# A hybrid decoder layer: the selected values of the NSA pages take another way into SBUF

## The chip, the cores and the metric

One core of one Trainium2 chip runs the whole program in one launch. The metric is the device time of that launch in microseconds; lower is better.

## The reference, cut to what matters

One decoder layer is computed for a prompt group (512 tokens) and a sample group (8 sequences, one new token each, 2048 cached positions in 16 pages of 128 rows). Between two large linear layers stand four mixers. Only the native sparse attention (NSA) of the sample group is touched by the change:

```
nsa_past = cache_nsa_kv[l, page_table].reshape(bs, past_len, 4, HEAD_DIM)   # [cmp_k, cmp_v, sel_k, sel_v]
kc, vc   = nsa_compress(rows[:, :, 0] / rows[:, :, 1], ...)                  # small MLP over 32-row blocks
imp      = importance of the 64-row blocks, from the compressed branch
p2       = masked_softmax(q . sel_k of the 16 chosen blocks)
o_sel    = p2 @ sel_v                                                       # the "selected values"
```

Each sequence thus reads, through the page table, 16 pages of four vectors of 64 floats a row. The compressed keys and values and the selected keys are needed early, the selected values only once the importance is known. MoBA, the second mixer with a paged cache, reads 4 x 256 KB of pages a unit, 32 units.

## The kernel before

The work is laid out as one list of steps, `timeline()` (TL). Every engine walks that list in order and does its own share of each step, so the list sets the order on each engine and semaphores tie the engines together. Where the list is merged from several streams, each step carries a due time, and the merge sorts by it.

**Panels.** The weights come as 89 panels of 512 KB (`load_panel`, three buffers `raw`). ScalarE casts a panel to a high part (L1258), VectorE (two of them GpSimd) forms the low part (L1630), TensorE multiplies (L793) and ScalarE or VectorE takes the sums out of PSUM. Panels 0 to 16 are the combined input projection, 17 to 24 the output projection, the rest the feed-forward part.

**NSA blocks.** Behind each of the panels 5 to 12 stands one step `nsa` (b = 0 to 7). SyncE loads the 16 pages of a sequence as 16 transfers of 96 KB (rows of 768 B: compressed pair and selected keys) into one half of `nsa_ring` (`load_nsa`, L660); the load of block n waits for the scores of block n-2. TensorE does `compress` (L820) and `sel_scores` (L839), ScalarE copies the sums to `hu` (L1290, L1291), VectorE adds (L1650), takes the row maximum (L1657) and subtracts (L1662), ScalarE takes the exponentials (L1296). GpSimd computes the pooling differences (`pdiff`, behind panels 8 and 10). Behind panel 12 ScalarE also takes out two convolution results (`cpw`, L1373), for which panel 13 waits; a little later (`zcols`, L1311) it writes `Vn`, whose space the gate weights `wgate` have held before.

**The merged stretch.** Behind panel 16 the last seven MoBA pairs (9 to 15), the prompt's attention columns, the joining of the statistics and the selected values are merged by due time. A MoBA pair is scores (`mu`, L1085), transpose (`mt`, L1092) and values (`mp`, L1097). Behind `mp` of pair n, SyncE loads unit 2n+4 and GpSimd unit 2n+5 (L629, L1546) for pair n+2: four transfers of 256 KB each, rows of 2 KB, each issuer waiting for `mp_mm`. The selected values come in 32 steps `selv`, six behind each pair: four transfers of 32 KB each with rows of 256 B, half of the steps on SyncE (L707), half on GpSimd (L1554), the page numbers read into registers first. They are read from a separate tensor `selv_pages` into eight buffers `selV[b]`, and the product with the probabilities (`spv`, L1150) follows from due time 37 on. A queue works in order, so a MoBA load stands behind the selv transfers that come before it in the list.

Of the kernel before, what the change touches and what calls it, by code (L numbers as in the profile page):

```python
# [5 lines left out]
F32 = mybir.dt.float32  # L6
# [4 lines left out]
ACT = mybir.ActivationFunctionType  # L11
# [3 lines left out]
P = 128  # L15
# [88 lines left out]
ROW_PIECES = (4, 9, 9, 6)  # L104
MB1, PAIR_T, SELV_T = 9, 9.1, 6
SELV_POOL = (1, 3, 5, 7)
SELV_AT = [8 * (_m // 8) + (_m % 8) // 2 + 4 * (_m % 2) for _m in range(4 * B)]
NCN = sum(c[0] != "moba" for c in COLS)
# [9 lines left out]
def timeline():  # L118
# [119 lines left out]
    for g in range(MB1, MB):  # L238
        at_ = 1 + PAIR_T * (g - MB1)
        units += [(at_, ("mu", g)), (at_ + 2.5, ("mt", g)), (at_ + 4.7, ("mp", g))]  # L240
        units += [(at_ + 4.6 * (m >= 4), ("selv", k)) for m, k in enumerate(SELV_AT[SELV_T * (g - MB1):SELV_T * (g - MB1 + 1)])]
    end = 1 + PAIR_T * (MB - MB1)
    join = [(8 + 2 * k, ("stat", k)) for k in range(5)] + [(18.5, ("comba", 0)), (19.8, ("combe", 0)), (22.3, ("comba", 1)), (23.9, ("comba", 2)), (27.4, ("backa", 0))]
    for b in range(B):
# [111 lines left out]
def build(nc, a, o):  # L356
    ctx = ExitStack()
    with ctx:
        def sem(name):
            return ctx.enter_context(nc.semaphore(name))  # L360
# [25 lines left out]
        w1 = place("w1", [P, 16, P])  # L386
        at[0] = o_a + 16384
        nsa_ring = place("nsa_ring", [P, 2, PAGES, 192])
        o_m = at[0]
# [7 lines left out]

        selV = [place(f"selV{b}", [P, PAGES, HD], F32, o_raw + ((OUT0 + b) % NRAW if b < NRAW else b) * PAGES * HD * 4 if b < B - 1 else o_op + (KT + 6) * NT * 4) for b in range(B)]
        WB = place("WB", [B, 11, P], F32, o_op + 2 * NT * 4)

# [73 lines left out]
        Vn = place("Vn", [P, 3, QT, P])  # L474
        wgate = place("wgate", [P, KT * GW], F32, o_vn)
        zs = place("zs", [B, 12, P])
        cst = place("cst", [P, NCONST])
# [75 lines left out]
        def bank_read(eng, k, step):  # L553
# [28 lines left out]
            sem("shift_h"), sem("cq_done"), sem("cexp_done"), sem("pv_done"), sem("o_done"), sem("pick_done"))  # L582
        shift_low = sem("shift_low_done")
        pool_d, pool_mm = sem("pool_d"), sem("pool_mm")
        cm_mm, csq_done, cv_mm, cn_done, cswish, cpw_mm = (
# [6 lines left out]
            sem("ms_mm"), sem("mmax"), sem("mt_mm"), sem("mp_mm"), sem("om_done"))  # L592
        stat_mm, comb_sub, comb_exp, wb_done, back_mm = (
            sem("stat_mm"), sem("comb_sub"), sem("comb_exp"), sem("wb_done"), sem("back_mm"))
        pscaled, st_mm, spv_mm, md_done, mpv_mm, fin_o, fin_mm = (
# [16 lines left out]
        def _(sp_):  # L612
# [19 lines left out]
            for kind, n, *part in TL:  # L632
# [21 lines left out]
                elif kind == "load_nsa":  # L654
                    if n == 1:
                        sp_.wait_ge(cmp_mm, 1)
                    if n >= 2:
                        sp_.wait_ge(ssel_mm, n - 1)
                    for p, v in enumerate(pages(n * PAGES, PAGES)):
                        sp_.dma_start(nsa_ring[:, n % 2, p, :],  # L660
                                      a["nsa_pages"][bass.ds(v, 1)].rearrange("a p n -> (a p) n")).then_inc(nsa_in[n % 2], 16)
                elif kind == "load_post":
                    sp_.wait_ge(ssel_mm, B)
                    sp_.wait_ge(kc_done, B + 1)
                    sp_.wait_ge(conv_done, 1)
# [62 lines left out]
        def _(pe):  # L728
# [220 lines left out]
            for step in TL:  # L949
# [187 lines left out]
                elif kind == "spv":  # L1137

                    b = n
                    if b == 0:  # L1140
                        read(pe, ACC[max(m for m in range(NACC1) if PAIR[m] == 1)])
                        mm(psum[:, 3, :], zeros[:, :], Psel[:, 0, :], start=True, stop=False, skip_group_check=True)
                    pe.wait_ge(selv_in[b], 16 * PAGES)
                    pe.wait_ge(win_in, 32)
# [79 lines left out]
        def _(act):  # L1224
# [13 lines left out]
            for step in TL:  # L1238
# [39 lines left out]
                elif kind in ("cmpp", "nsa"):  # L1278
                    idx = 0 if kind == "cmpp" else n + 1
                    m = NCMP if idx else NCMP_P  # L1280
                    act.wait_ge(cmp_mm, idx + 1)
                    if idx == 0:
# [24 lines left out]
                elif kind == "zcols":  # L1307
                    act.wait_ge(zc_mm, 1)
                    fn(gT[:, :, :], psum[:, 4, 0:QT * NGATE].rearrange("p (a b) -> p a b", a=QT), ACT.Tanh, scale=0.5).then_inc(gate_t, 1)
                    act.wait_ge(zc_mm, 2)  # L1310
                    fn(Vn[:, 0, :, :], psum[:, 5, :].rearrange("p (a b) -> p a b", a=QT), ACT.Copy).then_inc(vn_done, 1)  # L1311
                elif kind == "zrow":
# [79 lines left out]
                elif kind == "combe" and n == 0:  # L1392
                    act.wait_ge(comb_sub, 1)
                    fn(sm[:, 0:NGATE], zs[:, 0, 0:NGATE], ACT.Tanh, scale=0.5)
                    fn(eb[:, 2, :, 0:33], eb[:, 2, :, 0:33], ACT.Exp)
                    fn(eb[:, 2, :, 50:55], eb[:, 2, :, 50:55], ACT.Exp).then_inc(comb_exp, 1)
                elif kind == "combe" and n == 1:
                    act.wait_ge(comb_sub, 2)
                    fn(eb[:, 2, :, 33:50], eb[:, 2, :, 33:50], ACT.Exp).then_inc(comb_exp, 1)
                elif kind == "backa":  # L1400
# [80 lines left out]
        def _(pool):  # L1481
# [16 lines left out]
            for kind, n, *part in TL:  # L1498
# [40 lines left out]
                if kind == "mp" and 2 * n + 5 < MU:  # L1539
# [5 lines left out]
                    for j, v in enumerate(ids):  # L1545
                        pool.dma_start(moba_ring[q % 4][:, j, :],  # L1546
                                       a["moba_pages"][bass.ds(v, 1)].rearrange("a p n -> (a p) n")).then_inc(moba_odd[q % 4 // 2], 16)
                if kind == "selv" and n // 4 in SELV_POOL:

                    if n == 4:  # L1550
                        pool.wait_ge(mm_done, N_IN_PANELS)
                    pool.wait_ge(mp_mm, MB1 + SELV_AT.index(n) // SELV_T - 1)
                    for p, v in enumerate(pool_pages(n * 4), n * 4):
                        pool.dma_start(selV[p // PAGES][:, p % PAGES, :],  # L1554
                                       a["selv_pages"][bass.ds(v, 1)].rearrange("a p n -> (a p) n")).then_inc(selv_in[p // PAGES], 16)
                elif kind == "xsum":
# [40 lines left out]
        def _(dve):  # L1597
# [22 lines left out]
            for step in TL:  # L1620
# [81 lines left out]
                elif kind == "taps_s":  # L1702
                    if n == 0:
                        tmp = Vn[:, 0, :, :].rearrange("p a b -> p (a b)")[:, 0:B * CW].rearrange("p (b k) -> p b k", b=B)
                        for t in range(2):
# [167 lines left out]
                elif kind in ("comba", "combm"):  # L1873
# [6 lines left out]
                    if n == 0:  # L1880
# [21 lines left out]
                        for br, (lo, hi) in parts:  # L1902
                            last = tt(E[:, :, lo:hi], spread(MN[:, br, :], hi - lo), NM[:, :, lo:hi], ALU.subtract)
                        last.then_inc(comb_sub, 1)
                    elif n == 1:
                        if kind == "comba":
                            dve.wait_ge(comb_exp, 1)
                            ts(sm[:, 0:NGATE], sm[:, 0:NGATE], 0.5, 0.5, ALU.mult, ALU.add)
                        else:
                            dve.wait_ge(comb_exp, 2)  # L1910
                        for br, (lo, hi) in parts:
# [185 lines left out]
def layouts(x):  # L2097
# [86 lines left out]
    for n in range(2):  # L2184
# [6 lines left out]
        "w_gate": f(np.pad(panel(w_in, allr, r(c0[3], NGATE)), ((0, 0), (0, 0), (0, GW - NGATE))).reshape(P, KT * GW)),  # L2191
        "nsa_pages": f(np.concatenate([cmpT, selK], 2)),
        "selv_pages": f(nsa[:, :, 3]),
        "moba_pages": f(np.concatenate([mK, mV], 2)),
# [39 lines left out]
```

## Time and profile before

| | us |
|---|---|
| median of 3 runs | 766.06 |
| the three runs | 765.99, 766.06, 770.39 |
| profiled execution, device time | 770.32 |
| its span, first to last instruction | 768.6 |

| engine | busy us | share |
|---|---|---|
| TensorE (PE) | 737.8 | 96% |
| VectorE (DVE) | 429.2 | 56% |
| ScalarE (ACT) | 285.5 | 37% |
| GpSimd (POOL) | 210.4 | 27% |

The chain that ended last is 76% TensorE and 5% DMA, the largest DMA part being loads of MoBA pages. 113.49 MB move in all, 17,017 of the 63,980 packets being under 512 B. A span is the time from the first to the last instruction; the device time holds a little more. A timeline row gives the start, the time, the engine and the line, and in brackets how long the engine stood before it and what ended that. In a row of windows the DMA share is that of the 16 DMA engines, and PEclk is the granted TensorE clock as a share of full speed.

### The profile page before, as it was taken

The page shows a single profiled execution, that of the slowest core. Times are in us where ns is not written, and L with a number is a line of the kernel's source. Part 1 is how long each engine was busy: PE and PEld are TensorE (multiplying, and loading weights), DVE is VectorE, ACT ScalarE, POOL GpSimd, SP SyncE. Part 2 cuts the span into 40 slices and gives each one's busy share as a digit, 9 for nine tenths or more (in the row PEclk, how much of TensorE's full clock was granted, in tenths as well). Part 3 has the DMA queues.
Part 4 walks back from the last instruction along what each step waited for, and adds up shares of the span by engine and source line. Part 5 has one row for each costly group of instructions (what it writes and reads, how often), then busy time and mean ns, then how long its engine had stood idle before and what let it go on. Part 6 is the DMA issues. An engine that isn't in the chain of part 4 may idle for free.

```text
span 768.6 us, 17343 instructions
## 1 busy us (share of the span) xinstructions
PE 737.8 (96%) x6904; PEld 659.2 (86%) x6904; DVE 429.2 (56%) x740; ACT 285.5 (37%) x561; POOL 210.4 (27%) x284
## 2 busy tenths in 40 slices
PE   8999999998987899999999999999999999999997
PEld 7999989875563545589999999999999999999996
DVE  4878994665643532556866556433563355536355
ACT  5222334465553222533434454212341124324115
POOL 0000527024226772004747721001110012100433
PEclk9999999999999899999999999999999999999999
DMA  9656773378779996321332333322233323325002
GB/s 332 188 151 182 213 200 97 133 286 315 280 252 309 261 280 208 117 83 56 130 144 84 89 104 104 117 83 84 83 104 93 106 71 95 107 87 165 2 15 99
DMA packets 63980, 113.49 MB, mean 148 GB/s; under 512 B 17017, under 2 KB 36218, under 8 KB 63226
## 3 DMA queue, kind: packets, MB, share of 16 engines
q1 hardware_dynamic: 57370, 95.58, 39.9%
q0 software_dynamic: 6528, 16.78, 6.7%
q8 instruction: 55, 0.90, 0.5%
q14 instruction: 27, 0.22, 0.1%
HBM read 107.90 MB, written 6.52 MB: 149 GB/s over the span
## 4 chain that ended last, share of the span: by engine, by line
PE 76%; DVE 8%; DMA 5%; issue 5%; SPq 4%; ACT 3%; POOL 0%; ACTq 0%; DVEq 0%; POOLq 0%
PE psum L793 55%; DMA moba_hi<-in_moba_pages 4%; PE psum L812 4%; PE psum L820 3%; PE psum L899 2%; PE psum L933 2%; SPq L707 1%; PE psum L1085 1%; SPq L629 1%; PE psum L868 1%; PE psum L1097 1%; DVE yc L1700 1%; DVE wL L1630 1%; PE psum L1133 1%; DMA wgate<-in_w_gate 1%
## 5 line engine op out<-in xcount | busy, mean ns | idle before, releaser
L1630 DVE TENSOR_TENSOR wL<-raw,wH 128x1024 fp32r<-128x1024 f32 (+1 forms) x85 | 107.1, 1261 | 84.2 <-ACT wH L1258 84.2
L1258 ACT ACTIVATE wH<-raw 128x1024 fp32r<-128x1024 f32 (+1 forms) x87 | 88.8, 1021 | 103.1 <-PE psum L793 101.1
L793 PE MATMUL psum<-oxH,wH 128*128 128x260 f32 (+1 forms) x512 | 105.0, 286 | 0.7 <-DVE oxL L2054 0.5
L793 PE MATMUL psum<-oxH,wL 128*128 128x260 f32 (+1 forms) x512 | 103.9, 284 | 0.0
L793 PE MATMUL psum<-oxL,wH 128*128 128x260 f32 (+1 forms) x512 | 103.4, 283 | 0.0
L1592 POOL TENSOR_TENSOR hsq<-relu 128x520 f32<-128x520 f32 x32 | 33.8, 1055 | 217.9 <-ACT relu L1437 217.9
L793 PE MATMUL psum<-opH,wH 128*128 128x260 f32 x400 | 85.5, 295 | 5.2 <-DVE wL L1630 1.4
L793 PEld LDWEIGHTS psum<-oxH,wH 128*128 128x128 f32 x512 | 79.5, 189 | 2.5 <-issue 1.7
L793 PE MATMUL psum<-opL,wH 128*128 128x260 f32 x400 | 80.5, 283 | 0.0
L793 PE MATMUL psum<-opH,wL 128*128 128x260 f32 x400 | 80.5, 283 | 0.0
L793 PEld LDWEIGHTS psum<-oxL,wH 128*128 128x128 f32 x512 | 79.9, 190 | 0.0
L793 PEld LDWEIGHTS psum<-oxH,wL 128*128 128x128 f32 x512 | 79.4, 189 | 0.0
L793 PE MATMUL psum<-hidH,wL 128*128 128x260 f32 x384 | 77.4, 283 | 0.0
L793 PE MATMUL psum<-hidL,wH 128*128 128x260 f32 x384 | 77.3, 283 | 0.0
L793 PE MATMUL psum<-hidH,wH 128*128 128x260 f32 x384 | 77.2, 282 | 0.0
L793 PEld LDWEIGHTS psum<-opH,wH 128*128 128x128 f32 x400 | 61.6, 189 | 11.9 <-issue 4.0
L1437 ACT ACTIVATE relu<-relu,wcol 128x520 f32<-128x520 f32 x32 | 23.4, 731 | 112.0 <-DVE relu L2002 112.0
L793 PEld LDWEIGHTS psum<-opH,wL 128*128 128x128 f32 x400 | 61.8, 189 | 0.0
L793 PEld LDWEIGHTS psum<-opL,wH 128*128 128x128 f32 x400 | 61.7, 189 | 0.0
L793 PEld LDWEIGHTS psum<-hidH,wH 128*128 128x128 f32 x384 | 59.2, 189 | 0.0
L793 PEld LDWEIGHTS psum<-hidH,wL 128*128 128x128 f32 x384 | 59.2, 188 | 0.0
L793 PEld LDWEIGHTS psum<-hidL,wH 128*128 128x128 f32 x384 | 59.0, 188 | 0.0
(395 smaller groups left out, 1313.1 us busy)
## 6 DMA issues: line engine op xcount, KB each, us to landing
raw<-in_panels SPq DMA_DIRECT2D x88, 512.0 KB, 3.6
nsa_ring<-in_nsa_pages SPq DMA_DIRECT2D x128, 96.0 KB, 2.2
moba_hi<-in_moba_pages SPq DMA_DIRECT2D x36, 256.0 KB, 5.2
moba_lo<-in_moba_pages SPq DMA_DIRECT2D x36, 256.0 KB, 5.3
moba_hi<-in_moba_pages POOLq DMA_DIRECT2D x28, 256.0 KB, 5.1
moba_lo<-in_moba_pages POOLq DMA_DIRECT2D x28, 256.0 KB, 5.5
xres<-in_xT SPq DMA_DIRECT2D x8, 260.0 KB, 5.2
xres<-in_xT SPq DMA_DIRECT2D x1, 2080.0 KB, 8.6
```

The lines of the kernel that those rows point to most:

```text
L629: sp_.dma_start(moba_ring[q % 4][:, p, :], a["moba_pages"][bass.ds(v, 1)].rearrange("a p n -> (a p) n")).then_inc(moba_in[q % 4], 16)
L707: sp_.dma_start(selV[p // PAGES][:, p % PAGES, :], a["selv_pages"][bass.ds(v, 1)].rearrange("a p n -> (a p) n")).then_inc(selv_in[p // PAG ...
L793: last = mm(out[:, hf, 0:cols], w, x[:, k, hf * HALF:hf * HALF + cols], start=(t == 0 and j == 0), stop=(t == KT - 1 and j == 2))
L812: last = mm(psum[:, q % 4, 0:HALF], w[:, t, :], x[:, t, h * HALF:(h + 1) * HALF], start=(t == 0 and j == 0), stop=(t == KT - 1 and j == 2))
L820: last = mm(psum[:, 4, kv * 256:kv * 256 + n], w1[:, kv * 8 + r, :], rhs(kv, r), start=(r == 0), stop=(r == 7))
L868: mm(psum[:, b + e, 0:m], zT[base:base + HD, sq + t, i * P:(i + 1) * P], zT[base:base + HD, sk, 0:m], start=True, stop=False, skip_group_c ...
L899: mm(out[e], k, zT[base:base + HD, sq + t, lo:T], start=True, stop=False, skip_group_check=True)
L933: last = mm(psum[base:base + HD, 6 + t, lo:T], v, PT[0:keys, n % 2, e, 0:T - lo], start=COL_FIRST[n], stop=COL_LAST[n], skip_group_check=True)
L1258: fn(wtiles(0, n).rearrange("p a b -> p (a b)")[:, cols], raw[:, n % NRAW, cols], ACT.Copy).then_inc(h_done, 1)
L1437: fn(relu[:, up_no % 2, :], relu[:, up_no % 2, :], ACT.Relu, bias=wcol[:, up_no % 3, 0:1], scale=-1.0).then_inc(relu_done, 1)
L1592: nc.gpsimd.tensor_tensor(hsq[:, up_no % 2, :], relu[:, up_no % 2, :], relu[:, up_no % 2, :], ALU.mult).then_inc(sq_done, 1)
L1630: tt(wtiles(1, n).rearrange("p a b -> p (a b)")[:, cols], raw[:, n % NRAW, cols], wtiles(0, n).rearrange("p a b -> p (a b)")[:, cols].bitc ...
```

## The change

The fourth vector of each page row, the selected value, is appended to the NSA pages, so that a row has 1 KB and a page transfer 128 KB. `nsa_ring` grows by a third, into space behind `w1` that was free. In each `nsa` step ScalarE first waits for the pages and copies the 64 value columns of all 16 pages into one of two buffers `stage` (in the space of `Vn`); GpSimd then issues one transfer of 512 KB from `stage` to a DRAM tensor `selv_rows[b]`. The next load of the same ring half waits for the copy, ScalarE's copy of block n for the write of block n-2, and `zcols` for all eight writes. In the merged stretch one step `selv` for each sequence remains, on SyncE alone: one transfer of 512 KB, rows of 4 KB, with no page numbers, due at 1, 6, 11, ..., 36. GpSimd has no selv transfers left there. The temporary of `taps_s` moves, and two semaphores of the joining become one.

```diff
-MB1, PAIR_T, SELV_T = 9, 9.1, 6
-SELV_POOL = (1, 3, 5, 7)
+MB1, PAIR_T, SELV_T = 9, 9.1, 5
...
-        units += [(at_ + 4.6 * (m >= 4), ("selv", k)) for m, k in enumerate(SELV_AT[SELV_T * (g - MB1):SELV_T * (g - MB1 + 1)])]
     end = 1 + PAIR_T * (MB - MB1)
+    units += [(1 + SELV_T * b, ("selv", b)) for b in range(B)]
...
-        nsa_ring = place("nsa_ring", [P, 2, PAGES, 192])
+        nsa_ring = place("nsa_ring", [P, 2, PAGES, 256])
...
+        selv_rows = nc.dram_tensor("selv_rows", [B, P, PAGES, HD], F32, kind="Internal").ap()
+        stage = place("stage", [P, 2, PAGES, HD], F32, o_vn)
# SyncE, load_nsa
                     if n >= 2:
                         sp_.wait_ge(ssel_mm, n - 1)
+                        sp_.wait_ge(packed, n - 1)
# SyncE, selv
-                elif kind == "selv" and n // 4 not in SELV_POOL:
+                elif kind == "selv":
                     if n == 0:
                         sp_.wait_ge(mm_done, N_IN_PANELS)
-                    for p, v in enumerate(pages(4 * n, 4), 4 * n):
-                        sp_.dma_start(selV[p // PAGES][:, p % PAGES, :],
-                                      a["selv_pages"][bass.ds(v, 1)].rearrange("a p n -> (a p) n")).then_inc(selv_in[p // PAGES], 16)
+                        for done in selv_out:
+                            sp_.wait_ge(done, 16 * B // 2)
+                    sp_.dma_start(selV[n][:, :, :], selv_rows[n]).then_inc(selv_in[n], 16)
# ScalarE, nsa
+                    if idx:
+                        act.wait_ge(nsa_in[n % 2], 16 * PAGES * (n // 2 + 1))
+                        if n == 0:
+                            act.wait_ge(gate_mm, 1)
+                        if n >= 2:
+                            act.wait_ge(selv_out[n % 2], 16 * (n // 2))
+                        fn(stage[:, n % 2, :, :], nsa_ring[:, n % 2, :, 192:256], ACT.Copy).then_inc(packed, 1)
                     act.wait_ge(cmp_mm, idx + 1)
# ScalarE, zcols, ahead of the copy to Vn
+                    for done in selv_out:
+                        act.wait_ge(done, 16 * B // 2)
# GpSimd
-                if kind == "selv" and n // 4 in SELV_POOL:
...
+                if kind == "nsa":
+                    pool.wait_ge(packed, n + 1)
+                    pool.dma_start(selv_rows[n], stage[:, n % 2]).then_inc(selv_out[n % 2], 16)
```

## Rows read from the trace of the kernel before

**Rows 1.** Page of the profiled run, its first line
```profile
span 768.6 us, 17343 instructions
```

**Rows 2.** Windows, whole core, stage of the NSA pages; span, engines, PEclk, DMA share, GB/s
```profile
67.90:78.90 11.00, 11.00 (x102) 10.10 (x101) 10.56 (x19) 3.30 (x8) 0.00 (x0) 1.00 0.70 189
```

**Rows 3.** Timeline of SyncE's queue; start us, us, engine line op
```profile
55.90 9.45 SPq L660 DMA_DIRECT2D nsa_ring<-in_nsa_pages  x16
65.41 0.42 SPq L619 DMA_DIRECT2D raw<-in_panels  x1
67.02 9.22 SPq L660 DMA_DIRECT2D nsa_ring<-in_nsa_pages  x16
```

**Rows 4.** Chain of work that ended last; start us, us, what
```profile
72.35 3.77 PE psum L820 x32
```

**Rows 5.** Timeline of ScalarE, same stage
```profile
98.21 0.27 ACT L1290 ACTIVATE hu<-psum 64x127 f32<-64x127 f32 x1 [2.90 <-PE psum L820]
...
124.40 0.27 ACT L1290 ACTIVATE hu<-psum 64x127 f32<-64x127 f32 x1 [1.07 <-PE psum L820]
...
138.49 0.68 ACT L1358 ACTIVATE zT<-psum,vec 128x520 f32<-128x520 f32 x1
139.19 0.27 ACT L1290 ACTIVATE hu<-psum 64x127 f32<-64x127 f32 x1
...
143.50 1.06 ACT L1258 ACTIVATE wH<-raw 128x1024 fp32r<-128x1024 f32 x1
...
149.79 0.60 ACT L1311 ACTIVATE Vn<-psum 128x512 f32<-128x512 f32 x1 [0.28 <-PE psum L982]
```

**Rows 6.** Timeline of VectorE, the last NSA block
```profile
139.21 0.68 DVE L1669 TENSOR_REDUCE st<-Psel 128x8 f32<-128x512 f32 x1
```

**Rows 7.** Timeline of TensorE, panel 13 begins
```profile
143.66 0.51 PE L793 MATMUL psum<-opH,wH 128*128 128x260 f32 x2 [1.19 <-ACT zT L1373]
```

**Rows 8.** Windows, three stretches with different transfers
```profile
70.00:73.00 3.00, 3.00 (x24) 2.63 (x23) 2.86 (x5) 0.61 (x3) 0.00 (x0) 1.00 0.75 203
169.00:174.00 5.00, 5.00 (x72) 3.69 (x72) 2.46 (x8) 3.23 (x12) 2.77 (x2) 1.00 1.00 357
228.00:232.00 4.00, 3.20 (x54) 1.32 (x42) 2.86 (x9) 1.51 (x5) 2.15 (x4) 1.00 0.59 121
```

**Rows 9.** Timeline of SyncE's queue behind panel 16
```profile
230.93 4.58 SPq L629 DMA_DIRECT2D moba_hi<-in_moba_pages  x4
236.55 7.62 SPq L707 DMA_DIRECT2D selV<-in_selv_pages  x12
244.68 1.88 SPq L629 DMA_DIRECT2D moba_lo<-in_moba_pages  x4
...
254.89 2.65 SPq L629 DMA_DIRECT2D moba_hi<-in_moba_pages  x4
```

**Rows 10.** Timeline of GpSimd, same stretch
```profile
242.41 2.29 POOL L1546 DMA_DIRECT2D moba_lo<-in_moba_pages  x4 [0.41 <-issue]
```

**Rows 11.** Timeline of TensorE, same stretch
```profile
233.18 1.07 PE L1097 MATMUL psum<-moba_lo,PTm 128*32 128x256 f32 x16 [0.34 <-DVE PTm L1814]
...
243.35 1.93 PE L1085 MATMUL psum<-moba_hi,QM 128*32 128x128 f32 x32 [4.12 <-DMA moba_hi<-in_moba_pages]
...
253.74 1.08 PE L1085 MATMUL psum<-moba_lo,QM 128*32 128x128 f32 x32 [0.46 <-DMA moba_lo<-in_moba_pages]
...
264.28 1.94 PE L1085 MATMUL psum<-moba_hi,QM 128*32 128x128 f32 x32 [0.62 <-DMA moba_hi<-in_moba_pages]
```

**Rows 12.** Windows around two of these waits, with the granted clock
```profile
240.00:244.00 4.00, 0.65 (x14) 0.68 (x18) 0.00 (x0) 0.00 (x0) 3.36 (x7) 0.92 1.13 231
244.00:248.00 4.00, 4.00 (x40) 1.90 (x31) 0.87 (x5) 0.46 (x2) 3.01 (x7) 0.65 0.97 275
264.00:268.00 4.00, 3.72 (x46) 2.68 (x46) 2.59 (x7) 0.81 (x3) 3.18 (x6) 0.50 0.79 206
268.00:272.00 4.00, 4.00 (x23) 1.56 (x25) 0.92 (x3) 0.22 (x1) 3.26 (x7) 0.67 0.94 318
```

More of the change, by code:

```diff
@@ L104 @@
 ROW_PIECES = (4, 9, 9, 6)
-MB1, PAIR_T, SELV_T = 9, 9.1, 6
-SELV_POOL = (1, 3, 5, 7)
-SELV_AT = [8 * (_m // 8) + (_m % 8) // 2 + 4 * (_m % 2) for _m in range(4 * B)]
+MB1, PAIR_T, SELV_T = 9, 9.1, 5
 NCN = sum(c[0] != "moba" for c in COLS)
@@ L386, in build @@
         w1 = place("w1", [P, 16, P])
-        at[0] = o_a + 16384
-        nsa_ring = place("nsa_ring", [P, 2, PAGES, 192])
+        at[0] = o_a + 8192
+        nsa_ring = place("nsa_ring", [P, 2, PAGES, 256])
         o_m = at[0]
@@ L475, in build @@
         wgate = place("wgate", [P, KT * GW], F32, o_vn)
+        stage = place("stage", [P, 2, PAGES, HD], F32, o_vn)
+        taps_tmp = place("taps_tmp", [P, B, CW], F32, o_vn + 8192)
         zs = place("zs", [B, 12, P])
@@ L583, in build @@
         shift_low = sem("shift_low_done")
+        packed, selv_out = sem("selv_packed"), [sem(f"selv_written_back{i}") for i in range(2)]
         pool_d, pool_mm = sem("pool_d"), sem("pool_mm")
@@ L592, in build @@
             sem("ms_mm"), sem("mmax"), sem("mt_mm"), sem("mp_mm"), sem("om_done"))
-        stat_mm, comb_sub, comb_exp, wb_done, back_mm = (
-            sem("stat_mm"), sem("comb_sub"), sem("comb_exp"), sem("wb_done"), sem("back_mm"))
+        stat_mm, comb, wb_done, back_mm = (
+            sem("stat_mm"), sem("comb_sub_then_exp"), sem("wb_done"), sem("back_mm"))
         pscaled, st_mm, spv_mm, md_done, mpv_mm, fin_o, fin_mm = (
@@ L663, in _ @@
                     sp_.wait_ge(ssel_mm, B)
+                    sp_.wait_ge(packed, B)
                     sp_.wait_ge(kc_done, B + 1)
@@ L1142, in _ @@
                         mm(psum[:, 3, :], zeros[:, :], Psel[:, 0, :], start=True, stop=False, skip_group_check=True)
-                    pe.wait_ge(selv_in[b], 16 * PAGES)
+                    pe.wait_ge(selv_in[b], 16)
                     pe.wait_ge(win_in, 32)
@@ L1392, in _ @@
                 elif kind == "combe" and n == 0:
-                    act.wait_ge(comb_sub, 1)
+                    act.wait_ge(comb, 1)
                     fn(sm[:, 0:NGATE], zs[:, 0, 0:NGATE], ACT.Tanh, scale=0.5)
                     fn(eb[:, 2, :, 0:33], eb[:, 2, :, 0:33], ACT.Exp)
-                    fn(eb[:, 2, :, 50:55], eb[:, 2, :, 50:55], ACT.Exp).then_inc(comb_exp, 1)
+                    fn(eb[:, 2, :, 50:55], eb[:, 2, :, 50:55], ACT.Exp).then_inc(comb, 1)
                 elif kind == "combe" and n == 1:
-                    act.wait_ge(comb_sub, 2)
-                    fn(eb[:, 2, :, 33:50], eb[:, 2, :, 33:50], ACT.Exp).then_inc(comb_exp, 1)
+                    act.wait_ge(comb, 3)
+                    fn(eb[:, 2, :, 33:50], eb[:, 2, :, 33:50], ACT.Exp).then_inc(comb, 1)
                 elif kind == "backa":
@@ L1547, in _ @@
                                        a["moba_pages"][bass.ds(v, 1)].rearrange("a p n -> (a p) n")).then_inc(moba_odd[q % 4 // 2], 16)
-                if kind == "selv" and n // 4 in SELV_POOL:
[L1550 to L1555, printed above, removed]
+                if kind == "nsa":
+                    pool.wait_ge(packed, n + 1)
+                    pool.dma_start(selv_rows[n], stage[:, n % 2]).then_inc(selv_out[n % 2], 16)
                 elif kind == "xsum":
@@ L1703, in _ @@
                     if n == 0:
-                        tmp = Vn[:, 0, :, :].rearrange("p a b -> p (a b)")[:, 0:B * CW].rearrange("p (b k) -> p b k", b=B)
+                        tmp = taps_tmp[:, :, :]
                         for t in range(2):
@@ L1903, in _ @@
                             last = tt(E[:, :, lo:hi], spread(MN[:, br, :], hi - lo), NM[:, :, lo:hi], ALU.subtract)
-                        last.then_inc(comb_sub, 1)
+                        last.then_inc(comb, 1)
                     elif n == 1:
                         if kind == "comba":
-                            dve.wait_ge(comb_exp, 1)
+                            dve.wait_ge(comb, 2)
                             ts(sm[:, 0:NGATE], sm[:, 0:NGATE], 0.5, 0.5, ALU.mult, ALU.add)
                         else:
-                            dve.wait_ge(comb_exp, 2)
+                            dve.wait_ge(comb, 4)
                         for br, (lo, hi) in parts:
@@ L2191, in layouts @@
         "w_gate": f(np.pad(panel(w_in, allr, r(c0[3], NGATE)), ((0, 0), (0, 0), (0, GW - NGATE))).reshape(P, KT * GW)),
-        "nsa_pages": f(np.concatenate([cmpT, selK], 2)),
-        "selv_pages": f(nsa[:, :, 3]),
+        "nsa_pages": f(np.concatenate([cmpT, selK, nsa[:, :, 3]], 2)),
         "moba_pages": f(np.concatenate([mK, mV], 2)),
```

## The prediction

> **What bounds the kernel now.** The page gives the span [rows 1], and its chain of work is three quarters TensorE, so only a place where TensorE stands, or runs at less than its full clock, can give time back. I read the chain in order of time and found two stretches that the change touches. In the stage of the NSA pages (about 45 to 144 us) TensorE is busy for all of the 11.0 us of a block while the DMA engines carry 0.70 of what they can [rows 2]. There is little to win there, and the question is what the new work costs. Behind panel 16 (about 227 to 310 us) TensorE waits three times for MoBA pages, 4.12, 0.46 and 0.62 us [rows 11], beside a DMA share of about 1 [rows 12]. SyncE's queue shows why the later two are late: of `mp(9)`, which ends at 234.25 us [rows 11], the SyncE half of the reload goes out at 244.68, because 12 selv transfers taking 7.62 us stand before it [rows 9], and GpSimd's half at 242.41 [rows 10].
>
> **Part 1: rows of 1 KB instead of 768 B.** The number of transfers stays at 16 a block, so SyncE's issue (9.45 us in the busiest form [rows 3]) does not grow by itself; what grows is traffic. For one block before: 1.57 MB of pages at 203/0.75 = 271 GB/s [rows 8], 5.8 us, and a panel of 0.52 MB at 357 GB/s (2 KB rows [rows 8]), 1.5 us: 7.3 of 11.0 us, near the measured share of 0.70 [rows 2]. After: 2.10 MB at 271 (the price of the 768 B rows) to 357 GB/s (that of 2 KB rows), 7.7 to 5.9 us; the panel, 1.5; and the write of 0.52 MB at 357 down to 121/0.59 = 205 GB/s, the stretch in which outputs are written [rows 8], 1.5 to 2.6 us. Together 8.9 to 11.8 us in a block of 11.0. I take 10.3, the middle, since 1 KB lies between the two row lengths. The cover is the ring: the load for block 2 starts at 55.90 [rows 3] and TensorE needs it at 72.35 [rows 4], 16.45 us later. At 10.3 us nothing shows; at 11.8 the landing slips by 0.8 us a block, 4.0 over five further loads, against 16.45 - 11.8 = 4.65 of slack, so both ends cost 0. Later panels are loaded more than a block ahead.
>
> **Part 2: ScalarE's copy.** The price is that of a cast of the same 1024 elements a partition, 1.06 us [rows 5], eight times. In blocks 0 to 5 ScalarE stands 2.90 us for TensorE's sums right behind the place of the copy [rows 5], so it costs nothing; without that gap it would cost 1.06 each. In block 6 the gap is 1.07 us [rows 5], cost 0 to 0.1. In block 7 there is none: ScalarE finishes L1358 at 139.17 and goes to the `hu` copies at 139.19 [rows 5]. With the copy they start at 140.23, and VectorE's addition, free to start at 139.89 [rows 6], starts at 140.8 (0.56 us behind the first `hu` copy). All of what follows is serial: VectorE, ScalarE's L1373, and TensorE, which already stands 1.19 us for it [rows 7]. Cost 0.9; bounds 0.9 to 1.1. Part 2 costs 1.0 in all.
>
> **Part 3: the write back and the new waits.** Behind GpSimd's `packed` wait of block 3 stands `pdiff`, which starts some 2 us later and has more than a block of room. The write of block 4 then stands behind it, but is asked for only two blocks later. `zcols` is the tight one: the last copy ends at 140.2, and ScalarE needs the write landed ahead of L1311 at 149.79 [rows 5], moved to about 150.8. With an issue like GpSimd's of four transfers (2.29/4 = 0.6 us [rows 10]) and 0.52 MB at the slow 205 GB/s, 2.6 us, plus latency, it lands by about 146. Cost 0, up to 1 if latency is several us more.
>
> By the Trainium skill ("DMA: Bandwidth & Descriptors", the anatomy of a DMA on the GpSimd path) such a transfer takes about 2.0 us and its bytes at 436 GB/s, here 3.2 us: an estimate from the page, and it agrees that the write is in time.
>
> **Part 4: SyncE and GpSimd behind panel 16.** Removed: 64 transfers at about 7.62/12 = 0.63 us on SyncE [rows 9] and 64 at 0.57 on GpSimd [rows 10], with their page numbers. SyncE gets eight at about the same, 5 us in all. A MoBA reload now leaves right behind its `mp`, 8 to 10 us earlier for pair 11. The waits of 0.46 and 0.62 us go: 1.1 us. The large one at 243.35 us is for the pages of pair 10, and these were not behind selv transfers: SyncE issued them at 230.93, taking 4.58 us against 1.88 for the four at 244.68 [rows 9], for the engines were full with outputs and pages. What competed behind 236 us were the selv transfers of GpSimd; these go, but GpSimd's own four pages for pair 11 (1 MB, rows of 2 KB, 2.9 us of the DMA at 357 GB/s) move from 242.41 to about 234.5, into the same jam. From -4.1 (nothing competes) to +1.0 (the megabyte costs more than it replaces); I take -1.5, nearer to no change, because the same pages still wait behind the same outputs.
>
> **Part 5: the granted clock.** Around the long wait the clock is at 0.65 of full for 4.00 busy us, so 1.4 us lost; it falls again behind the small wait at 264 us: 0.50 of 3.72 and 0.33 of 4.00, 3.2 us lost [rows 12]. These are times at the lower level (0.5, that is 1.2 of 2.4 GHz) mixed with the full one. The first stays as long as TensorE stands there. Before the second, TensorE stood only 0.62 us for DMA [rows 11], and the small transposes beside it remain; I take half, -1.6, bounds 0 and -3.2.
>
> **Sum.** +1.0 - 1.1 - 1.5 - 1.6 = -3.2 us. The profiled execution takes 770.32 us, 1.7 more than its span [rows 1], and lies 4.3 above the median of 766.06, so part of its losses may be peculiar to it; still I subtract the whole sum: 766.06 - 3.2 = **762.9 us**.
>
> **Rivals.**
> *Full relief.* The long wait goes (-4.1), the two others (-1.1), both losses of clock (-1.4, -3.2), against +1.0: -8.8, **757.3 us**. For it: a wait of 4 us that ends in a DMA while small packets fill the engines. Against: the jam is made of outputs and pages that stay. Chance 0.18.
> *The wait only changes its cause.* GpSimd's pages for pair 11 take the share that selv had, the stand at 243 us stays, and with it both losses of clock: -1.1 + 1.0, **766.0 us**. For it: at 236 us about half of SyncE's outputs and pages are still to move, and GpSimd's megabyte arrives in a queue of its own. Chance 0.22.
>
> The Trainium skill ("DMA: Bandwidth & Descriptors", queues, rings and completion order) says that a DMA engine goes round between the queues that have work, packet by packet; by that rule the second queue takes half, and this rival is the outcome. The sum above, with its -1.5, stands between.
>
> *The ring runs dry.* Pages, panels and writes mixed run no faster than the mixture at 240 us, 231/1.13 = 204 GB/s [rows 12]: 3.15 MB a block take 15.4 us. It decides from 11.0 + 4.65/5 = 11.9 us a block; midway, at 13.7, five loads slip 2.7 us each, less 4.65 of slack, +8.9: 766.06 - 3.2 + 8.9 = **771.8 us**, at 15.4 us 780. For it: every sequence moves 1 MB more. Against: the mixture at 240 us held 256 B rows, which this stage does not have. Chance 0.10.
>
> **How the numbers follow.** The forecast has 0.50, the rivals 0.18, 0.22 and 0.10. A difference of 1% (7.7 us) is about what a measurement tells from none. The range runs from 757 (full relief) to 769.5: the forecast without its two estimated gains gives 766.0, and I add the 4.3 us between the runs seen in part, for three runs can fall on either side. Faster by over 1% is most of full relief, if it also frees what I left: 0.17. Slower by over 1% needs a block of about 14 us: 0.07. The rest, 0.76, is within 1%.
>
> **What would show it.** Right: TensorE still busy throughout the NSA blocks, DMA share above 0.9; TensorE's wait for L1373 near 2.1 us; reloads issued right behind `mp`; the waits at `mu` of pairs 11 and 12 gone, that of pair 10 about 2.6 us; the clock at the start of pair 12 higher in some part. Wrong: TensorE waiting for `nsa_ring`, ScalarE waiting ahead of L1311, a write landing over 9 us after its copy, or new waits for `moba_lo` because transfers of 512 KB now stand before them.

## The result, and the profile after

| | median us | runs |
|---|---|---|
| kernel before | 767.84 | 20 |
| changed kernel | 770.69 | 20 |

The ratio is 1.0036 with a 95% interval of 1.0021 to 1.0050: the change costs 0.4%, some 2.8 us, where I had forecast a gain of 3.2. The two profiled executions hide this: 770.32 us before, 769.31 after. One slow run of each kernel (1173.42 and 779.14 us) is left out of the ratio and of the ranges that follow. The single runs of either kernel spread over several microseconds (765.99 to 772.48 before, 765.26 to 774.96 after), so one execution can't decide a difference of this size, and the verdicts below rest on the ratios of many runs. The starting point moved too: the median of three runs from which I subtracted was 766.06 us, that of twenty is 767.84. The profiles serve to say where a wait is and what ended it.

The page of the changed kernel; the row of packets stood at 113.49 MB before, with 17,017 of them under 512 B:

```profile
span 767.5 us, 16965 instructions
...
PE 738.7 (96%) x6904; PEld 659.4 (86%) x6904; DVE 429.7 (56%) x740; ACT 293.0 (38%) x569; POOL 179.5 (23%) x228
...
DMA packets 55017, 121.84 MB, mean 159 GB/s; under 512 B 7034, under 2 KB 26235, under 8 KB 54267
```

The packets under 512 B fell by 9,983, and 8.35 MB came. The window of the changed kernel that answers to [rows 2], with the same columns, shows where:

```profile
67.90:78.90 11.00, 11.00 (x102) 10.10 (x102) 10.58 (x19) 4.25 (x9) 0.53 (x1) 1.00 0.90 276
```

DMA share 0.90 at 276 GB/s. The ring loads answer to [rows 3], here SyncE's queue of the changed kernel, and under them the one wait of TensorE for the ring in its waits (us in total, times, longest):

```profile
57.29 9.95 SPq L663 DMA_DIRECT2D nsa_ring<-in_nsa_pages  x16
...
69.05 9.63 SPq L663 DMA_DIRECT2D nsa_ring<-in_nsa_pages  x16
...
80.41 9.11 SPq L663 DMA_DIRECT2D nsa_ring<-in_nsa_pages  x16
...
92.71 8.09 SPq L663 DMA_DIRECT2D nsa_ring<-in_nsa_pages  x16
```

```profile
PE psum L824 <- DMA nsa_ring<-in_nsa_pages: 0.7, 1, 0.7
```

The loads start 11.4 to 12.3 us apart, 11.8 on average from block 2 to block 6, where the kernel before has 10.6 to 11.5 and 11.0 on average. By block 5 TensorE is short of pages. The end of the stage answers to [rows 5, 7], ScalarE and then TensorE of the changed kernel:

```profile
138.83 0.69 ACT L1371 ACTIVATE zT<-psum,vec 128x520 f32<-128x520 f32 x1
139.40 1.06 ACT L1291 ACTIVATE stage<-nsa_ring 128x1024 f32<-128x1024 f32 x1
140.49 0.27 ACT L1301 ACTIVATE hu<-psum 64x127 f32<-64x127 f32 x1
```

```profile
144.93 0.51 PE L797 MATMUL psum<-opH,wH 128*128 128x260 f32 x2 [2.11 <-ACT zT L1386]
```

The copy takes 1.06 us and TensorE's wait grows from 1.19 to 2.11 us, both as forecast. What I had not counted stands in the windows behind it, first the changed kernel, then the kernel before:

```profile
144.00:148.00 4.00, 3.07 (x12) 2.40 (x13) 1.82 (x2) 2.21 (x5) 0.00 (x0) 0.67 0.00 0
148.00:152.00 4.00, 4.00 (x31) 3.35 (x30) 0.49 (x2) 0.00 (x0) 0.00 (x0) 0.50 0.74 256
```

```profile
144.00:148.00 4.00, 4.00 (x42) 3.29 (x41) 2.20 (x3) 0.94 (x3) 0.00 (x0) 1.00 0.33 98
148.00:152.00 4.00, 4.00 (x42) 3.83 (x42) 2.37 (x9) 1.22 (x3) 0.00 (x0) 1.00 0.95 370
```

Behind the longer wait the granted clock is 0.67 and then 0.50, the lower of its levels (1.2 GHz), and work that took 4 us takes up to 8. The first MoBA scores show what was lost by then, in the changed kernel and in the kernel before:

```profile
163.36 1.08 PE L1089 MATMUL psum<-moba_hi,QM 128*32 128x128 f32 x32
```

```profile
159.13 1.08 PE L1085 MATMUL psum<-moba_hi,QM 128*32 128x128 f32 x32
```

They start 4.2 us later. From the start of panel 13 it is 18.4 us instead of 15.5, so 2.9 us of the 4.2 lie behind the wait. Behind panel 16 this execution gets them back. TensorE of the changed kernel at pairs 9 and 10, to be held against [rows 11]:

```profile
233.77 1.69 PE L1089 MATMUL psum<-moba_lo,QM 128*32 128x128 f32 x32 [2.79 <-DMA moba_lo<-in_moba_pages]
...
244.65 1.08 PE L1089 MATMUL psum<-moba_hi,QM 128*32 128x128 f32 x32
```

The 4.12 us at pair 10 are gone, but pair 9 waits 2.79 us for pages, which it did not in the profile before, and pair 10 starts 1.3 us later than in the kernel before. The pages of pair 10 did not come sooner. TensorE came later: its `mp(9)` starts at 238.68 us instead of 233.18 [rows 11]. (Pair 9 waits 0.3 to 2.5 us for pages in each of the twelve profiles of the experiments, those with the small transfers too, so not all of the 2.79 belongs to the change.)

### The profile page after: what moved, and what is told of

It reads as the page before. It is cut to its first block, busy times and chain, and to the rows that moved or that the text cites. A ratio compares the mean times of both kernels' runs of the same rounds, so it can differ in the third digit from the quotient of the medians.

```text
span 767.5 us, 16965 instructions
## 1 busy us (share of the span) xinstructions
PE 738.7 (96%) x6904; PEld 659.4 (86%) x6904; DVE 429.7 (56%) x740; ACT 293.0 (38%) x569; POOL 179.5 (23%) x228
## 4 chain that ended last, share of the span: by engine, by line
PE 72%; DVE 7%; issue 6%; SPq 5%; DMA 5%; ACT 4%; POOL 1%; POOLq 0%; ACTq 0%; DVEq 0%
PE psum L797 51%; PE psum L816 4%; SPq L663 4%; PE psum L903 2%; DMA moba_lo<-in_moba_pages 2%; PE psum L937 2%; DMA moba_hi<-in_moba_pages 2%; PE psum L1101 1%; PE psum L824 1%; PE psum L1089 1%; PE psum L872 1%; DMA nsa_ring<-in_nsa_pages 1%; DMA wgate<-in_w_gate 1%; SPq L625 1%; PE psum L1154 1%
## 5 line engine op out<-in xcount | busy, mean ns | idle before, releaser
L797 PEld LDWEIGHTS psum<-opH,wH 128*128 128x128 f32 x400 | 62.0, 190 | 11.4 <-issue 4.0
```

The lines of the kernel that those rows point to most:

```text
L797: last = mm(out[:, hf, 0:cols], w, x[:, k, hf * HALF:hf * HALF + cols], start=(t == 0 and j == 0), stop=(t == KT - 1 and j == 2))
```

## The experiments

I had two theories. **A**: the NSA stage costs much more than 1 us, through the place of the last copy and the clock behind it, and the late part gives back some. **B**: the late part's relief is chance of one profile. Ratios are always against runs of the kernel before on the same chip. Each version has 12 runs, the one with all four moves 8, and the last late part, the doubled copy and the changed kernel's repeat 6 each.

### The two halves apart

The late part alone, on the kernel before:

```diff
-    units += ... ("selv", k) ...                 # 32 steps of 4 x 32 KB on SyncE and GpSimd
+    units += [(1 + SELV_T * b, ("selv", b)) for b in range(B)]
...
+                    sp_.dma_start(selV[n][:, :, :], a["selv_rows"][n]).then_inc(selv_in[n], 16)
```

> The kernel before with only the merged stretch of the change: the selected values come as eight loads of 512 KB with rows of 4 KB from a ready-made DRAM tensor (the first 128 pages instead of those of the page table, so the selected values are those of other rows); no copy, no write back, rows of 768 B in the ring as before. Theory: this part gives 3 to 5 us (the waits of TensorE for pages of pairs 10 to 12 gone), so the kernel is about 0.5% faster than before. Rival (the relief seen in one profile is chance, the loads of 512 KB only take the place of the small ones): within 1 us of the kernel before.

Measured: 0.9995 (0.9973 to 1.0016). The rival held: this part is worth nothing that can be told. TensorE at pair 10 of this kernel, and GpSimd's reload for pair 11:

```profile
244.28 1.53 PE L1081 MATMUL psum<-moba_hi,QM 128*32 128x128 f32 x32 [4.55 <-DMA moba_hi<-in_moba_pages]
```

```profile
235.44 2.29 POOL L1542 DMA_DIRECT2D moba_lo<-in_moba_pages  x4 [3.53 <-PE psum L1093]
```

With no small transfer left, the wait at pair 10 is 4.55 us against 4.12 [rows 11]. GpSimd's megabyte for pair 11 now leaves at 235.44 instead of 242.41 [rows 10], into the time in which the pages of pair 10 are still on their way. The small waits were not made by the small transfers either: with all of these in place, rows of 1 KB alone, the NSA part alone and copies and writes alone show no wait for pages at pairs 11 and 12, where the kernel before had 0.46 and 0.62 us.

The NSA part alone, on the changed kernel, with the selected values loaded as before:

```diff
-                    sp_.dma_start(selV[n][:, :, :], selv_rows[n]).then_inc(selv_in[n], 16)
+                    for p, v in enumerate(pages(4 * n, 4), 4 * n):    # the loads of the kernel before, SyncE and GpSimd
+                        sp_.dma_start(selV[p // PAGES][:, p % PAGES, :], a["selv_pages"][...])
```

> The changed kernel with the selected values loaded in the merged stretch as before, from their own tensor in rows of 256 B: rows of 1 KB in the ring, ScalarE's copies and GpSimd's writes stay, and nobody reads what was written. Theory: this part costs 6 to 8 us against the kernel before (0.9 of longer wait at panel 13, 3 of clock behind it, the rest from the ring and what follows). Rival, as forecast: 1 us.

Measured: 1.0042 (1.0018 to 1.0066), 3.2 us: the whole loss, though half of what I expected. The halves add up: 1.0042 x 0.9995 = 1.0037 against 1.0036 for the change. Its profile shows both marks again, TensorE 2.11 us ahead of panel 13 and 1.5 us for the ring, and the clock at 0.53 from 148 to 152 us.

### The NSA part taken to pieces

Rows of 1 KB alone, on the kernel before:

```diff
-        nsa_ring = place("nsa_ring", [P, 2, PAGES, 192])
+        nsa_ring = place("nsa_ring", [P, 2, PAGES, 256])
...
-        "nsa_pages": f(np.concatenate([cmpT, selK], 2)),
+        "nsa_pages": f(np.concatenate([cmpT, selK, nsa[:, :, 3]], 2)),
```

> The kernel before with rows of 1 KB in the NSA ring and nothing else: no copy, no write, selected values as before. SyncE's sixteen page loads in the changed kernel start 11.8, 11.4 and 12.3 us apart where the kernel before has 11.1, and TensorE waits 0.7 us for the ring once. Theory (traffic of rows of 1 KB alone makes the load period exceed the block): the load period is 11.4 us or more here too and the time 1 us above before. Rival (the write back makes the difference): period 11.1 us, time the same as before within 0.5 us.

Measured: 1.0005 (0.9989 to 1.0022). The loads start at 55.78, 66.80, 77.83, 89.04 and 99.91 us, as before, and TensorE never waits for the ring. The rival held: traffic of 241 GB/s at a share of 0.82 (50 to 110 us) stays hidden.

Copies and writes alone, rows of 768 B:

```diff
+                        fn(stage[:, n % 2, :, :], nsa_ring[:, n % 2, :, 128:192], ACT.Copy).then_inc(packed, 1)
...
+                    pool.dma_start(selv_rows[n], stage[:, n % 2]).then_inc(selv_out[n % 2], 16)
```

> The kernel before with ScalarE's eight copies and GpSimd's eight writes of 512 KB added, rows of 768 B in the ring as before (the copy takes the selected keys' columns, and nobody reads what was written). With rows of 1 KB alone the time was 1.0005 of the kernel before, with rows, copies and writes 1.0042. Theory (the copy of block 7 carries it: TensorE stands 2.1 us ahead of panel 13 and runs at half clock behind it): about 1.003 here, the wait for the convolution outputs 2.1 us, no wait of TensorE for the ring, and SyncE's ring loads 11.0 us apart. Rival (only rows of 1 KB and writes together fill the DMA engines and that carries it): 1.001.

Measured: 1.0032 (1.0007 to 1.0057), as the theory has it, but for the spacing: the ring loads start at 56.45, 67.64, 79.06 and 91.73, up to 12.7 us apart, without TensorE running dry. The share of the DMA engines is 0.80 here (50 to 110 us), less than with rows of 1 KB alone, where the loads kept to 11.0 us. So the copies and writes space the loads, and not the fullness of the DMA engines by itself.

The same with the last copy moved behind the two convolution outputs:

```diff
-                    if idx:
+                    if idx and n < B - 1:
                         act.wait_ge(nsa_in[n % 2], 16 * PAGES * (n // 2 + 1))
...
                 elif kind == "cpw":
...                                                     # both convolution outputs first
+                    fn(stage[:, (B - 1) % 2, :, :], nsa_ring[...], ACT.Copy).then_inc(packed, 1)
```

> The kernel before with the eight copies and eight writes (rows of 768 B, columns of the selected keys, nobody reads what was written), the copy of block 7 behind the convolution outputs. With that copy in its place the time was 1.0032. Theory (the place of the last copy is what costs): 1.000 to 1.001, the wait ahead of panel 13 at 1.2 us. Rival (the traffic of the writes costs, not the place of a copy): 1.003.

Measured: 1.0002 (0.9983 to 1.0021). TensorE at panel 13, first with the copy in its place, then with the copy moved:

```profile
144.11 0.51 PE L799 MATMUL psum<-opH,wH 128*128 128x260 f32 x2 [2.11 <-ACT zT L1388]
```

```profile
143.28 0.51 PE L799 MATMUL psum<-opH,wH 128*128 128x260 f32 x2 [1.19 <-ACT zT L1388]
```

So of the 1.0032 nearly all, 0.3% or 2.3 us, hangs on the place of one copy of 1.06 us, though the intervals of the two overlap, and the two versions ran on different chips, each beside the kernel before there. The longer wait itself is 0.92 us of it.

The same move in the changed kernel:

> The changed kernel, with ScalarE's copy of the last NSA block moved behind the two convolution outputs (L1386) for which panel 13 waits. The trace of the changed kernel has TensorE standing 2.11 us there against 1.19 before, and then 6 to 8 us at half clock (granted clock 0.67 and 0.50 from 144 to 152 us), which the kernel before does not have. Theory (the late cost is this copy): the wait returns to about 1.2 us, the clock between 144 and 152 us is 1.00 again, and the time falls by 3 to 4 us against the changed kernel, to about 1 us below the kernel before. Rival (the cost is the ring loads, which run later by the block, and TensorE starved of pages): the time falls by 1 us at most and stays 2 us above the kernel before.

Measured: 1.0011 (0.9988 to 1.0034); the wait is 1.19 us again and the windows from 144 to 152 us show 1.00. Against 1.0036 that is 0.25%, about 1.9 us: less than the 3 to 4 of the theory, more than the rival's 1, and the two intervals overlap. The kernel does not get below the one before. Its profile also answers what became of the wait at pair 10. Here the selected values come as in the changed kernel, the NSA stage ends on time, and the long wait is back:

```profile
242.96 1.75 PE L1089 MATMUL psum<-moba_hi,QM 128*32 128x128 f32 x32 [4.89 <-DMA moba_hi<-in_moba_pages]
```

The dose doubled, the last copy done twice in its place:

```diff
+                        if n == B - 1:
+                            chain(fn(stage[:, n % 2, :, :], nsa_ring[:, n % 2, :, 192:256], ACT.Copy))
                         fn(stage[:, n % 2, :, :], nsa_ring[:, n % 2, :, 192:256], ACT.Copy).then_inc(packed, 1)
```

> The changed kernel with the copy of block 7 done twice in its place. Theory (each microsecond there is on the path, and the longer wait lets the clock fall more often): the wait ahead of panel 13 is 3.2 us, and the time 1 to 3 us above the changed kernel, 1.005 to 1.007 of the kernel before. Rival (the MoBA loads behind absorb what is lost there): the same time as the changed kernel within 0.5 us.

> The changed kernel itself once more, for a second profile. Its first showed the granted clock at 0.67 and 0.50 from 144 to 152 us. Theory: TensorE waits 2.1 us ahead of panel 13 again (this is order of work, not chance), the ring loads start 11.4 us or more apart, the time is 1.003 to 1.004. Whether the clock falls behind the wait is open: it fell in two profiles of three with this wait.

Measured: 1.0070 (1.0049 to 1.0090) with two copies, 1.0063 (1.0039 to 1.0087) for the changed kernel itself beside it, so the price of the second copy can't be told: the step is within the spread, and the experiment is inconclusive on it. On this same chip the version with copies, writes and the last copy moved came to 1.0002 (0.9983 to 1.0021), and there the intervals lie apart from both. (The changed kernel's 1.0063 lies above its first 1.0036, and above the 1.003 to 1.004 expected; the intervals meet at 1.004 to 1.005, and the first rests on 20 runs, the second on 6.) The wait did grow as expected, and the clock behind it fell, in the profile of the two copies:

```profile
145.51 0.80 PE L797 MATMUL psum<-opH,wH 128*128 128x260 f32 x2 [3.20 <-ACT zT L1388]
```

```profile
148.00:152.00 4.00, 4.00 (x30) 3.46 (x29) 0.25 (x1) 0.38 (x2) 0.00 (x0) 0.50 0.52 168
```

The second profile of the changed kernel has 0.61 and 0.54 in the two windows and 0.6 us of wait for the ring. Of the clock the profiles say this. With a wait of 2.1 us or more ahead of panel 13 it reached 0.50 to 0.54 in four of five (not in the one with copies and writes alone). With 1.2 us it stayed at 1.00 in seven of nine, and in two (rows of 1 KB, late part alone) was 0.70 to 0.72 and then 0.85 to 0.88. That is frequency in fourteen executions, not a rule. The price of a fall can be read off: from the start of panel 13 to the first MoBA scores TensorE takes 15.5 us in the eight profiles whose clock stayed at 1.00, 17.0 in the two with a partial fall, and 18.4 in the four with a full one, the doubled copy among them. A full fall costs 2.9 us, a partial one 1.5.

How often it falls shows in the runs as well, for each has its mean granted clock over the whole span. It is 0.991 in 55 runs of the five kernels with the longer wait (0.990 to 0.992 by kernel), and 0.994 both in 36 runs of the three with the copy moved (0.992 to 0.995) and in 82 runs of the kernel before. The 0.003 between them, times a span of 768 us, are some 2.3 us, an estimate. With the 0.9 of wait that makes 3.2, near the 2.8 us between the mean times of these 55 and 36 runs (771.1 and 768.3). A mean over the span does not say where the clock was lost; the profiles put it behind panel 13.

SyncE reading its page numbers ahead of its waits, with the copy moved:

```diff
+                    ids = pages(n * PAGES, PAGES)
                     if n == 1:
                         sp_.wait_ge(cmp_mm, 1)
...
-                    for p, v in enumerate(pages(n * PAGES, PAGES)):
+                    for p, v in enumerate(ids):
```

> The changed kernel with the copy of block 7 behind the convolution outputs, and with SyncE reading the sixteen page numbers of a block ahead of its waits instead of behind them. Theory (the ring loads fall behind because 1 to 2 us of reading page numbers stands between the wait and the first transfer): the loads start within 0.3 us of the end of the scores, TensorE does not wait for the ring at block 5, and the time is 1 us below that with the copy moved alone, equal to the kernel before. Rival (the DMA engines are full, 0.88 of their time, so an earlier issue only waits in the queue): the same wait of 1 us, the same time.

Measured: 1.0002 (0.9980 to 1.0025). TensorE does not wait for the ring (with the copy moved alone it waited 1.0 us at block 5), and the time is equal to the kernel before. But the loads start at 55.35, 68.07, 79.99, 92.88 and 104.83 us: the first is 0.2 us behind the end of the scores, as the theory has it, the others 1.9 to 5.6 us behind (the changed kernel has 69.05, 80.41, 92.71 and 104.59). The doubled copy, which reads its page numbers behind the waits, shows no wait for the ring either. So it is not shown that the reading ahead took the wait away, and the step from 1.0011 is smaller than the intervals.

### What the pages of pair 10 wait for

On the kernel before, one step of SyncE moved:

```diff
-... ("prep", 0), ("lsetl", 0), ("out_z", 0), ("vrow", 0), ...
+... ("prep", 0), ("lsetl", 0), ("vrow", 0), ...
...
+     join += [..., (end + 1.5, ("out_z", 0)), ...]
```

> The kernel before with one step moved: SyncE's four output transfers out_z (1.56 MB), which stand ahead of the reload for pair 10, go out behind the last MoBA pair. In the kernel before and in the late part alone TensorE waits 4.1 and 4.5 us for the pages of pair 10, with the small selv transfers and without them. Theory (the pages wait behind the outputs): that wait falls below 1 us and the kernel is 3 to 4 us faster. Rival (the pages of pair 10 come late whatever stands before them, for the MoBA reloads themselves fill the engines): the wait stays above 3 us, the time within 1 us.

Measured: 0.9948 (0.9928 to 0.9968), 4.0 us faster. SyncE's queue and TensorE of this kernel:

```profile
226.99 1.88 SPq L629 DMA_DIRECT2D moba_hi<-in_moba_pages  x4
229.38 8.35 SPq L707 DMA_DIRECT2D selV<-in_selv_pages  x12
238.23 1.88 SPq L629 DMA_DIRECT2D moba_lo<-in_moba_pages  x4
```

```profile
239.09 1.08 PE L1085 MATMUL psum<-moba_hi,QM 128*32 128x128 f32 x32
...
258.66 1.53 PE L1085 MATMUL psum<-moba_hi,QM 128*32 128x128 f32 x32 [1.39 <-DMA moba_hi<-in_moba_pages]
```

The reload for pair 10 leaves 1.3 us behind the start of `mp(8)` (225.72 us) instead of 3.5, and in 1.88 instead of 4.58 us [rows 9], and TensorE finds its pages. The selv transfers still stand there, 8.35 us of them in front of the next reload. That settles it: the long wait of [rows 11] was made by the four outputs, 1.56 MB. Whether by their bytes or by the 2 us that SyncE takes to issue them ahead of the reload, this run doesn't separate. Nor do all waits go: pair 9 waits 2.48 us and pair 12 1.39 in this profile.

Then the late part once more, with outputs and selected values both out of the way, first without the NSA part, then as the changed kernel with all four moves (last copy late, page numbers ahead, outputs late, selected values late):

```diff
-    units += [(1 + SELV_T * b, ("selv", b)) for b in range(B)]
+    units += [(24 + 2 * b, ("selv", b)) for b in range(B)]
```

> The late part alone (eight loads of 512 KB from a ready-made tensor, the first 128 pages instead of those of the page table; no copy, no write, rows of 768 B) with the outputs out_z behind the last pair and these loads due at 24 to 38. Beside the kernel before with the outputs moved, which came to 0.9948, this tells what removing the small selv transfers is worth once the pages of pair 10 no longer wait behind the outputs. Theory (the outputs hid the gain): 0.992, a further 2 us, TensorE's wait at pair 12 (1.4 us with the outputs moved alone) gone. Rival (the small transfers never cost anything): 0.995.

Measured: 0.9937 (0.9916 to 0.9957). Pairs 10 and 12 start without a wait, pair 9 waits 2.11 us. Against 0.9948 that is 0.1%, less than the intervals: it can't be told whether the small transfers cost anything.

> The same with two more moves: the outputs out_z behind the last pair, and the eight loads of selected values due at 24, 26, ..., 38 instead of 1, 6, ..., 36, so that only MoBA pages are on their way at pair 10. Theory: the wait at pair 10 goes, and the time is 4 to 5 us below the kernel before and 1 us or more below the one with the outputs moved alone. Rival (the late part has nothing to give beside the outputs): the same time as the kernel before with the outputs moved.

Measured: 0.9921 (0.9893 to 0.9950), a median of 761.81 against 768.27 us. This version is faster than the kernel before beyond its interval, and so than the changed one. TensorE at pairs 10, 11 and 12:

```profile
240.51 1.08 PE L1090 MATMUL psum<-moba_hi,QM 128*32 128x128 f32 x32 [0.67 <-DMA moba_hi<-in_moba_pages]
...
248.76 1.08 PE L1090 MATMUL psum<-moba_lo,QM 128*32 128x128 f32 x32
...
258.61 1.08 PE L1090 MATMUL psum<-moba_hi,QM 128*32 128x128 f32 x32
```

Its edge over the kernel before with the outputs moved (0.9948) lies within the two intervals, so most of the gain belongs to the outputs, and the change itself, put right, is at best worth the rest. GpSimd's megabyte for pair 11 leaves early here too, at 235.55 us, and pair 10 waits 0.67 us only: without the outputs the megabyte does not hold it up.

Of the two theories B held, and A held but for its last clause: the NSA stage costs 3.2 us, through the place of one copy and the clock behind it, and the late part gives back nothing that can be told.

## Why the prediction was wrong

The forecast was -3.2 us and the change costs 2.8, 6.0 us apart. Parts 4 and 5 had promised 4.2 us, of which the late part alone shows 0.4 (0.9995); Parts 1 to 3 had 1.0 us for the NSA part, which took 3.2. The other 1.8 us between 762.9 and 770.69 are the starting point, three runs at 766.06 for twenty at 767.84.

**Part 1 (rows of 1 KB, cost 0)** was right for the traffic: 1.0005 for the rows alone, and a share of 0.90 where I had reckoned 10.3 of 11.0 us. It was wrong on the slack, which I thought enough even at 11.8 us a block. The load for block 2 started 1.4 us later than in [rows 3], for SyncE took 2.2 us over its page numbers, as the chain of the changed kernel shows:

```profile
54.90 2.22 SPq L625
```

The load for block 5 then started 3.3 us later than before, and its last page landed 5.6 us after its issue; I had counted the traffic of a block but no latency on top. So TensorE waited 0.7 us.

**Part 2 (the copies, 1.0 us)** is a failed term. Copy, place and wait came out to 0.1 us (wait +0.92 for my 0.9). What was missing is the granted clock behind it. I priced the clock only in Part 5, as something that could be won back, and never asked whether a wait that grows from 1.19 to 2.11 us could lose it elsewhere. With and without the copy in its place the ratios are 1.0032 and 1.0002 in one setting, 1.0036 and 1.0011 in the other: 2 us instead of 0.9. The rest is the clock: a full fall costs 2.9 us and came in four of five profiles, and the mean clock of 55 runs against 36 gives some 2.3 us. That the wait brings the fall about is shown only so far, that moving the copy took away both; the doubled copy did not give a second point.

**Part 3 (write back and waits, cost 0)** held. `pdiff` started 1.8 us later, the writes landed 2.9 to 6.9 us after their issue (median 5.1, above the estimate of 3.2), and ScalarE did not stand ahead of `Vn` for them. With the last copy moved, copies and writes came to 1.0002.

**Part 4 (late part, -2.6 us)** is the failed step that turned the sign. The -1.1 for the two small waits took them for the work of the small transfers; three other profiles with these transfers don't have them, so they were features of one execution. The -1.5 at the long wait was wrong: 4.55 us stayed in place of 4.12, and 4.89 with the whole change when the NSA stage was on time. I had named the reason, since those pages were not behind selv transfers but behind outputs, and still gave it a gain by standing between two cases. The moved outputs show that the other case was the whole of it: the wait stays as long as the outputs stand there. The Trainium skill's rule ("DMA: Bandwidth & Descriptors", queues, rings and completion order) that a DMA engine goes round between its queues pointed the same way. The trace agrees in so far as the wait stayed at 4.55 us with GpSimd's megabyte leaving early, at 235.44; no run here held that megabyte back by itself, and with the outputs gone it left early and did no harm (0.67 us).

**Part 5 (clock, -1.6 us)** fell with it. The late part alone still shows a clock of 0.90 from 232 to 248 us, as the kernel before does at 0.89. The dip at 264 us in [rows 12] is not in it, and the profile with rows of 1 KB only has less of it (0.89 from 264 to 280 us in place of 0.79), so it was largely a feature of the one execution that I had read. The profiled run lay 4.3 us above its median; I noted that and subtracted its losses from the median all the same.

Of the rivals, "the wait only changes its cause" described the late stretch, at 766.0 us with a chance of 0.22, though its cause, GpSimd's pages, is not what the runs show. The ring ran dry by 0.6 to 1.5 us in four of the five profiles with rows, copies and writes (and page numbers read behind the waits), not by 8.9. None had the clock behind panel 13, and with the low starting point that put the median at 770.69, above my range of 757 to 769.5.

## What to carry to other kernels

Before pricing a transfer's relief, find what stands directly in front of the late bytes in their own queue; here that was 1.56 MB of outputs that no engine waits for until some 120 us later, and moving them gave 0.5% where the redesign cost 0.4%. A microsecond added on a serial link between two engines is dearer than its length if TensorE stands for it, for the clock can fall behind a wait: put such work behind the instruction that TensorE waits for. And do not take the losses of one profiled execution off the median when that execution is slower than the median.

## What the runs showed of the hardware

- With GpSimd's first write of 512 KB on its way, SyncE's reading of sixteen page numbers took 2.2 us in the changed kernel, and its load for block 2 started at 57.29; with rows of 1 KB and no write it started at 55.78. The longest such reading step is 1.9 to 2.8 us in all nine profiles with copies and writes and 1.2 us in all five without. The copies and the writes were not tested apart, and the readings of the later blocks took 0.97 us beside writes too.
- Mixed traffic without 256 B rows ran at 394 GB/s at a share of 1.04 (240 to 244 us of the changed kernel), with them at 231 GB/s and 1.13 in the same stretch of the kernel before [rows 12]. Yet removing them gained nothing that can be told, since the bytes in front were others.
- Behind a TensorE wait of 2.1 us or more at panel 13 the granted clock fell to 0.50 to 0.54 in four of five profiles, and each such fall cost 2.9 us; behind 1.2 us it did so in none of nine.
